# RWKV chunk matrices of one decoder block on TensorE: 64x64 blocks in place of 128x128 block-diagonal ones

## The reference, cut to what matters

```
p = token_shift_lerp(xn @ w_in);  r, k, v, decay, a, kk from p      # 8 heads of 64
def step(S, inp):                                # per head, S is 64x64
    r_t, w_t, k_t, v_t, a_t, b_t = inp           # a_t = -kk, b_t = kk*a
    Sa = einsum('bhvk,bhk->bhv', S, a_t)
    S  = S * w_t + Sa * b_t + v_t * k_t          # outer products
    return S, einsum('bhvk,bhk->bhv', S, r_t)    # y_t
y = scan over 256 tokens
y = (y - mean(y)) * rsqrt(var(y) + LNX_EPS) * lnx_w + lnx_b   # mean and var per head
y = (y + sum(r*k*r_k) * v) * g
merged = sum over 3 branches of sigmoid(xn @ w_gate[b]) * (y_b @ w_branch[b]);  h = x + merged @ w_out
h = h + sparse_moe(rms_norm(h));  out = rms_norm(h)
```

## Time and profile before

| what | value |
|---|---|
| median of 3 runs | 1401.48 us (1398.84 to 1402.33) |
| the profiled execution: span, first to last instruction | 1400.3 us (the page gives no other time for it) |
| TensorE busy | 1345.4 us, 96% of the span |
| VectorE, ScalarE busy | 304.7 us, 199.0 us |
| DMA over the span | 449.68 MB, mean 321 GB/s |
| granted TensorE clock, mean | 0.978 of 2.4 GHz |

### The profile page before, as it was taken

The page is one execution under the profiler, slowest core; times in us unless marked ns, Lnnn a source line. Parts: engine busy times, 40 slices in busy tenths (PEclk is TensorE's granted clock), DMA queues, the critical chain, the costliest instruction groups (busy, mean ns, idle before and its releaser), DMA issues.

```text
span 1400.3 us, 15803 instructions
## 1 busy us (share of the span) xinstructions
PE 1345.4 (96%) x6334; PEld 668.9 (48%) x6334; DVE 304.7 (22%) x477; ACT 199.0 (14%) x382; POOL 0.2 (0%) x4
## 2 busy tenths in 40 slices
PE   7999999999999999999999999999999999999995
PEld 6886799888845333233233333323333333332321
DVE  1256564241111101111011110111201112011112
ACT  1234421110011010011100111001111001110002
POOL 0000000000000000000000000000000000000000
PEclk9999999999997899999999999999999999999998
DMA  9343100159454899999999999999999999999993
GB/s 340 113 169 104 47 1 1 61 185 393 158 203 173 340 417 418 417 416 416 418 418 418 417 418 416 417 418 418 418 418 417 417 418 418 417 419 415 415 416 126
DMA packets 95164, 449.68 MB, mean 321 GB/s; under 512 B 8529, under 2 KB 20945, under 8 KB 62193
## 3 DMA queue, kind: packets, MB, share of 16 engines
q1 hardware_dynamic: 94828, 448.00, 80.0%
q10 hardware_dynamic: 292, 1.07, 0.2%
HBM read 447.99 MB, written 1.05 MB: 321 GB/s over the span
## 4 chain that ended last, share of the span: by engine, by line
PE 87%; DMA 5%; DVE 4%; issue 1%; SPq 1%; ACT 1%; PEldq 0%; DVEq 0%
PE ps L447 84%; DMA ring<-in_w_exp 3%; DMA upper<-in_w_exp 2%; PE ps L906 1%; SPq L412 1%; DVE upper L1414 1%; PE ps L665 1%; SPq L404 1%; DVE ring L1329 0%; PE ps L917 0%; DMA xrows<-in_x 0%; ACT ring L1106 0%; PE ps L463 0%; DVE ring L1419 0%; DVE ring L1420 0%
## 5 line engine op out<-in xcount | busy, mean ns | idle before, releaser
L447 PE MATMUL ps<-ring,upper 128*64 128x512 f32 (+4 forms) x2656 | 604.6, 579 | 10.6 <-PE ps L447 4.3
L447 PEld LDWEIGHTS ps<-ring,upper 128*64 128x64 f32 (+2 forms) x2656 | 207.8, 144 | 379.7 <-issue 362.5
L447 PE MATMUL ps<-upper 128*64 128x512 f32 (+6 forms) x1544 | 287.8, 459 | 7.1 <-PE ps L447 4.3
L447 PEld LDWEIGHTS ps<-upper 128*64 128x64 f32 (+3 forms) x1544 | 145.7, 166 | 144.8 <-issue 136.6
L447 PE MATMUL ps<-xT,ring 128*128 128x256 f32 x672 | 150.7, 382 | 0.0
L447 PEld LDWEIGHTS ps<-xT,ring 128*128 128x128 f32 x672 | 127.2, 191 | 19.3 <-issue 2.3
L1581 DVE TENSOR_TENSOR xrows<-xrows,ps 128x1024 f32<-128x1024 f32 x32 | 39.1, 1221 | 352.2 <-PE ps L447 352.2
L1565 DVE TENSOR_SCALAR upper<-ps 128x512 f32<-128x512 f32 x32 | 22.1, 691 | 420.7 <-PEq L886 420.7
L1204 ACT ACTIVATE upper<-upper 128x512 f32<-128x512 f32 x32 | 20.2, 630 | 536.9 <-DVE upper L1565 536.9
L447 PE MATMUL ps<-merged,cst 1*64 1x512 f32 x256 | 66.2, 633 | 0.0
L1210 ACT ACTIVATE factors<-ps 64x512 f32<-64x512 f32 x64 | 37.9, 591 | 199.5 <-PEq L901 198.8
(11 more groups left out here) (199 smaller groups left out, 521.8 us busy)
## 6 DMA issues: line engine op xcount, KB each, us to landing
ring<-in_w_exp SPq DMA_DIRECT2D x288, 1024.0 KB, 19.3
upper<-in_w_exp SPq DMA_DIRECT2D x96, 1024.0 KB, 19.2
ring<-in_w_gate SPq DMA_DIRECT2D x9, 1024.0 KB, 4.9
ring<-in_w_in SPq DMA_DIRECT2D x8, 896.0 KB, 11.6
ring<-in_w_in SPq DMA_DIRECT2D x8, 640.0 KB, 3.9
ring<-in_w_branch SPq DMA_DIRECT2D x5, 1024.0 KB, 5.1
ring<-in_w_mem_kv SPq DMA_DIRECT2D x4, 1024.0 KB, 4.9
ring<-in_w_out SPq DMA_DIRECT2D x4, 1024.0 KB, 13.2
```

Of the source, the lines that this page charges most:

```text
L447: return pe.matmul(o, l, r, start=start, stop=stop, skip_group_check=True)
```

## The change

The off-diagonal halves are no longer stored or multiplied. Chunk c of a token tile lies on partitions 64c to 64c+63 and every head is a block of 64 columns. Every product of the stage is a 64x64 tile of the array, in an order (`corners`) that goes through the array's four quarters. The inverse's level 0 is transposed by VectorE (32x32 blocks), and so is the last operand before level 5. The state is 64 columns wide. `y` is made in token layout, normed there by VectorE with reductions, then transposed back on TensorE; the norm's weight and bias are applied by ScalarE in the copy from PSUM. `ar` has three parts, so that one matmul gives a x state and r x state together. `WIDE_AT` and the waits of the first DMAs into these slots follow the new layout.

```
-WIDE_AT = (8, 72, 80, 88, 96, 0, 16, 24, 32, 40)
+WIDE_AT = (88, 96, 8, 72, 80, 0, 16, 24, 32, 40)
...
                 elif s == NARROW:
-                    sp.wait_ge(t1_ps, 4 * (LEVELS - 1))
-                elif s == NARROW + 1:
-                    sp.wait_ge(yh_ps, 2)
+                    sp.wait_ge(pv_sb, 4)
+                elif s == NARROW + 2:
+                    sp.wait_ge(xx_ps, 2 * (LEVELS - 1))
+                elif s == NARROW + 3:
+                    sp.wait_ge(y_ps, NCH)
                 elif s == NARROW + 5:
-                    sp.wait_ge(y_rwkv_sb, 1)
+                    sp.wait_ge(y_rwkv_sb, TT)
...                                                    TensorE: gram, own values, inverse
-            for g in range(4):
...
-                    mm(ps[:, n % 6, 0:T], bT[b:b + 64, i, ts], ar[b:b + 64, i, :, ts])
-                    mm(ps[:, n % 6, T:2 * T], kT[b:b + 64, i, ts], ar[b:b + 64, i, :, ts], False).then_inc(gram_ps, 1)
+            corners = ((0, 0), (1, 1), (0, 1), (1, 0))
+            for n in range(4):
+                t, q = n // 2, n % 2
+                for i in range(2):
+                    for x, src in enumerate((bT, kT)):
+                        for a, c in corners:
+                            toks = slice(t * P + c * CH, t * P + (c + 1) * CH)
+                            last = mm(ps[rows64(c), 2 * n + a, (2 * i + x) * P:(2 * i + x + 1) * P],
+                                      src[rows64(a), 2 * q + i, toks], ar[rows64(a), (2 * q + i) * NCH + 2 * t + c, 1:3, :], i == 0 and x == 0)
+                last.then_inc(gram_ps, 1)
+            pe.wait_ge(gram_sb, 2)
+            own_values(0, 0)                 # 16 matmuls 64x64x64
+            pe.wait_ge(gram_sb, 3)
+            pe.wait_ge(inv0_sb, 1)
+            turn_inverse(0)                  # 4 transposes 128x128
+            pe.wait_ge(gram_sb, 4)
+            own_values(1, 6)
+            pe.wait_ge(inv0_sb, 2)
+            turn_inverse(1)
             for j in range(1, LEVELS):
...
+                    for h in range(HP):
+                        for c, a in corners:
+                            last = mm(ps[rows64(a), 2 * t + c, h * 64:(h + 1) * 64], gram[rows64(c), 2 * t + h // 2, a, h % 2, 0, 0, :],
+                                      inv[rows64(c), t, h, a, :], h == 0)
+                    last.then_inc(t1_ps, 1)
                     if j > 1:
+                        turn_inverse(t)
+                for t in range(TT):
+                    pe.wait_ge(t1_sb, 2 * (j - 1) + t + 1)
+                    pe.wait_ge(turned_sb, 2 * (j - 1) + t + 1)
...                                                    16 matmuls again, x = invT_a x t1s
...                                                    TensorE: one chunk of the recurrence
+                if ch:                        # waits: s_sb, and y_sb (invT_sb, twin_sb for ch 1)
+                    for hp in range(HP):
+                        for a in range(2):
+                            last = mm(ps[:, bank + a, hp * 64:(hp + 1) * 64], ar[rows64(a), hp * NCH + ch, 1 - e:3 - e, :],
+                                      state[rows64(a), ch % 2, hp, :], hp == 0)
+                    last.then_inc(r_ps, 1)
+                if ch < NCH - 1:              # 8 matmuls ktok x vtok
                 fill((ch, "a"))
+                for h in range(HR):           # 8 matmuls invT x rs_, 8 gram x vtok
                 fill((ch, "b"))
                 pe.wait_ge(u_sb, ch + 1)
+                if ch < NCH - 1:              # 8 matmuls btok x us, then s_ps
+                for h in range(HR):           # 8 matmuls gram x us, then y_ps
                 fill((ch, "c"))
...
-            fill("mean") ... mm(ps[:, b, :], heads, yT[:, 2 * b:2 * b + 2, :]) ... fill("var") ... mm(ps[:, b, :], heads, sqr[...])
+            fill("norm0")
+            pe.wait_ge(y_sb, 3)
+            pe.wait_ge(ynorm_sb, 1)
+            turn_y(0)                         # 4 transposes
+            fill("norm1")
+            pe.wait_ge(ynorm_sb, 2)
+            turn_y(1)
             fill("rest")
...                                                    VectorE: gram and level 0, last level
+            for n in range(4):
+                dve.wait_ge(gram_ps, n + 1)
+                TTn(gram[:, n]..., ps[:, 2 * n:2 * n + 2, :]..., const("causal")..., ALU.mult).then_inc(gram_sb, 1)
+                link(TTn(base, gram[:, n, :, :, 0, 0, :]..., const("level0t")..., ALU.mult))
+                link(TTn(base..., base..., const("eye")..., ALU.add))
+                if n % 2:
+                    dve.transpose(flat(inv[:, t]), flat(invT[:, t])).then_inc(inv0_sb, 1)
...
+                if j == LEVELS - 2:
+                    for t in range(TT):
+                        step(dve.transpose(flat(invT[:, t]), flat(inv[:, t])))
...                                                    VectorE: norm in token layout
+            def norm(t):
+                dve.wait_ge(y_sb, 2 * t + 2)
+                link(dve.tensor_reduce(stat[:, 3 * t, :], yh, AX.X, ALU.add))
+                link(TS(stat[:, 3 * t, :], stat[:, 3 * t, :], 1.0 / 64, None, ALU.mult))
+                link(TTn(yh, yh, stat[:, 3 * t, :]..., ALU.subtract))
+                link(TTn(sh, yh, yh, ALU.mult))
+                dve.tensor_reduce(stat[:, 3 * t + 1, :], sh, AX.X, ALU.add).then_inc(var_sb, 1)
+                dve.wait_ge(var_root, t + 1)
+                link(dve.reciprocal(stat[:, 3 * t + 2, :], stat[:, 3 * t + 1, :]))
+                TTn(yh, yh, stat[:, 3 * t + 2, :]..., ALU.mult).then_inc(ynorm_sb, 1)
```

More of the change, by code:

```diff
@@ L71 @@
 _at = 0
-for _n, _w in (("ident", P), ("heads", P), ("causal", 2 * P), ("level", LEVELS * P), ("level0t", P), ("before", P),
+for _n, _w in (("ident", P), ("heads", P), ("causal", P), ("level", LEVELS * CH), ("level0t", CH), ("eye", CH), ("before", P),
                ("ones", P), ("dist", 2 * P), ("iota", T), ("resets", T)):
@@ L111, in fill_points @@
 def fill_points():
-    points = [(ch, s) for ch in range(NCH) for s in "abc"] + ["mean", "var", "rest"]
+    points = [(ch, s) for ch in range(NCH) for s in "abc"] + ["norm0", "norm1", "rest"]
     counts = [1] * (3 * NCH) + [2, 3]
@@ L669, in _ @@
[L669 to L681 removed]
+            pe.wait_ge(pv_sb, 4)
@@ L713, in _ @@
[L713 to L720, removed]
+                        if t == 0:
+                            pe.wait_ge(av_sb, 2)
+                    else:
+                        pe.wait_ge(inv_sb, 2 * (j - 2) + t + 1)
@@ L722, in piece @@
+            pe.wait_ge(av_sb, 4)
             def piece(p):
@@ L758, in _ @@
             for ch in range(NCH):
-                t, c = ch // 2, ch % 2
-                rs = slice(64 * c, 64 * c + 64)
+                t, e = ch // 2, ch % 2
+                own, other = rows64(e), rows64(1 - e)
                 toks = slice(ch * CH, (ch + 1) * CH)
+                bank = 2 * (ch % 2)
                 if ch:
                     pe.wait_ge(s_sb, ch)
-                for hp in range(HP):
-                    last = mm(ps[rs, 0, hp * P:(hp + 1) * P], ar[:, hp, 0, toks], state[:, ch % 2, hp, :], hp == 0)
@@ new lines, in _, with turn_y @@
+                for h in range(HR):
+                    last = mm(ps[other, bank + h % 2, (h // 2) * 64:(h // 2 + 1) * 64], gram[own, 2 * t + h // 4, h % 2, h // 2 % 2, 0, 1, :],
+                              us[own, t, h * 64:(h + 1) * 64], False)
+                last.then_inc(y_ps, 1)
+                fill((ch, "c"))
+            def turn_y(t):
+                for f in range(HP):
+                    last = pe.transpose(ps[:, t, f * P:(f + 1) * P], ytok[:, t, f * P:(f + 1) * P], ident)
+                last.then_inc(yT_ps, 1)
@@ L1492, in _ @@
-            merge(after[0])
-            dve.wait_ge(var_root, 1)
-            link(dve.reciprocal(sqr, sqr))
-            link(TTn(yc, yc, sqr, ALU.mult))
-            for f in range(HP):
-                step(TS(yc[:, f, :], yc[:, f, :], col("lnw", f), col("lnb", f), ALU.mult, ALU.add))
-            settle()
-            link(TTn(yc, yc, bonus, ALU.add))
-            TTn(gT, gT, yc, ALU.mult).then_inc(y_rwkv_sb, 1)
-            for m in after[1:] + list(range(N_FILL, len(UNITS))):
+            norm(1)
@@ L1502, in _ @@
+            merges_of("norm0")
+            finish(0)
+            merges_of("norm1")
+            finish(1)
+            after = [p // PIECES for p in points["rest"] if p % PIECES == 5]
+            for m in after + list(range(N_FILL, len(UNITS))):
                 merge(m)
```

336 lines of the change are left out of this document (166 added, 170 removed).

## The result

| | median us | lowest to highest | runs |
|---|---|---|---|
| before | 1401.33 | 1398.84 to 1402.33 | 4 |
| changed | 1353.88 | 1353.18 to 1354.34 | 4 |

The ratio is 0.965 (95% interval 0.961 to 0.969): 47.5 us faster. The prediction had 1378 us and a range from 1363; the gain is twice what was forecast, and outside its range. In a second set of runs the changed kernel had 1351.9 us against 1401.1, ratio 0.964 (0.961 to 0.968). Profiled spans: 1400.3 us before, 1351.4 us after. Over all sets, 6 of the 37 executions of the kernel before took 1410 to 1412 us at a mean granted clock of 0.970 or lower; the medians hardly feel them, but a profile can be of such an execution, as e3's is.

What follows compares the result with a forecast made beforehand. TensorE was taken to bound the kernel until the expert stream restarts. Gram stage and inverse 14.3 plus recurrence 9.1 made 23.4 us, from 1400.3 to 1376.9 us of span, 1378 us median; 8-in-10 range 1363 to 1399.

Steps and rivals of the forecast that it cites:

- What bounds the kernel: TensorE bounds the first half, the expert stream the second; a microsecond saved before the stream's restart is one at the end.
- Gram stage: Gram stage and level 0: VectorE becomes the bound, TensorE needs 6.4 us; level 1 starts at 176.7 us against 180.3.
- The price of a 64x64 tile: Time per record on TensorE: 50 ns for alternating tiles, bounds 30 and 61; 61 for tiles in one row half.
- Inverse: Levels 1 to 5 take 7.4 us each against 9.06; recurrence starts 14.3 us earlier, gram stage's 3.6 included.
- Recurrence: Recurrence and norm: 22.3 us against 31.4 for the changed products, 9.1 us less, bounds 9.7 and 5.6.
- The end of the range: Fast end of the forecast: all tiles at the low ends save 36 us, giving 1365 us; range from 1363.
- Rival 1: Clock falls to 0.50 with small tiles; if held through the inverse, 37 us more, 1415 us; chance 0.08.
- Rivals 2 to 4: No overlap of small tiles, about 1440 us (0.04); half gain, 1393 us (0.12); no change, 1401 us (0.06).
- The floors: Possible floors on TensorE matmul starts: about 25 ns, a level of 4.2 us, or about 62 ns, 8.9 us.

Runs made afterwards that it cites:

- e3: Kernel before, with only the inverse's t1 products as two 64x64 tiles on the diagonal: 1396.1 us against 1401.7, ratio 0.9955; its profiled execution took 1408.0 us.
- e1: Changed kernel with long groups of 64x64 tile matmuls on one, two or four quarters added ahead of the recurrence, results unused: 1397.1 us.
- e5: Changed kernel with six idle products put into TensorE's two waits of the gram stage: 1350.3 us, ratio to before 0.9634.
- e8: Changed kernel with every gram product issued twice in the gram stage: 1352.5 us.
- e9: Changed kernel with half-tile groups and longer quarter groups added ahead of the recurrence: 30 ns a record for the column pair; no total given.
- a0: The changed kernel run once more, unaltered, as base for later runs: 1351.9 us, ratio to before 0.9641.
- e2: Changed kernel with the inverse's loops over quarters and heads swapped, four matmuls in a row on one quarter: 1363.7 us.
- e10: Changed kernel with the quarter order in gram stage and inverse altered so neighbours share a row half: 1355.1 us in one run.
- e4: Changed kernel with the wide slots in the order of before, and the waits that go with it: 1351.4 us, ratio 0.9655.
- e6: Changed kernel with the recurrence's r in four quarters and b'u mixed with the y products: 1350.8 us, ratio to before 0.9639.

## Why the prediction was wrong, step by step

- **What bounds the kernel**: right. Restart and end moved together by 48.0 and 48.9 us; e1 shows the same for 43 us added.
- **Gram stage**: 12.5 us forecast and measured, in part by luck. At full clock the stage lasts 11.8 us (e5); the low clock, which the forecast did not have, added 0.7. That VectorE bounds it was right (e8), TensorE's 6.4 us were too many (3.72 us for its 128 records). VectorE's transposes, which no row had shown, take 0.71 us (I took 0.69, with 3.3 as the far end).
- **The price of a 64x64 tile**: this is the step that failed. It said "Lower end: 118 / 4 = 30 ns. Upper end for alternating tiles: 61, if what I see there is a floor of two instructions a record [...] I take 50". Long runs give 15.9 ns, groups in the kernel 20. Two faults. The 61 ns in the earlier trace rows was the stream of 128 columns over two halves; e9 measures 30 ns on the same halves with 64. And the lower end divided the wrong thing: 118 ns for weights of 64 columns in one half was again the stream of 128 columns. The same form costs 59 with 64 columns, and 59 over four quarters is 15. I had written that load and stream both halve and that neighbours lie in other rows and columns, which is a factor of eight from a full tile's 118, and then divided by four.
- **Inverse**: the mechanism held, the size did not. With 20 ns a level is 2.5 + 1.2 + 0.2 = 3.9 us. The stage is 17.3 us shorter than forecast, of the 25.5 us by which the span beat the forecast gain of 23.4; the pause of 0.9 us (below) is inside.
- **Recurrence**: the same term, 6.3 us of the 25.5. 288 records at 41 ns on the average (11.8 us) in place of 61 (17.6 us); `r` 65 ns against 73. I had put these tiles at 61 because they lie in one half of the rows; but k'v, and `u` with the own y part, go to both column halves, that is to two quarters, where e1 has 30 ns, and they took 39 and 34.
- **The end of the range**: "All tiles at the low ends: 1365 us" took the wrong floor, so the range could not hold 1354.
- **Rival 1, the clock**: the fall exists, but it is short: from 173.4 to 176.6 us in the changed kernel's trace, half a microsecond into level 1, and up to about 178.5 us in a0's. The other levels ran at full clock. It cost about 1 us (e5 against a0).
- **Rivals 2 to 4**: not so. Of TensorE's waits in the inverse the largest is 0.41 us, inside level 5 and behind VectorE's transposes; in the level shown it is 0.15. And the stretch behind the norm is as long as before (144.7 against 145.1 us), so its weights do not come late.
- **The floors**: from "TensorE: Matmul & The Clock Gate" of the Trainium skill (the part on 56 ns against 53.3 ns) I named floors of 25 and 62 ns between starts, with estimates of 4.2 and 8.9 us a level. Neither binds here: 15.9 ns a record, weight load and stream, in four quarters (e1), and 3.93 us a level. Where the page and the measurement differ, the measurement holds. The same page of the Trainium skill has the rule that was missing, in its Part 3: matmuls whose tiles lie in other row and column groups run at the same time, with some 4 ns between starts. e1 agrees in kind (16, 30, 59 ns for four, two, one). In the changed kernel's `u` two records in different quarters start 0.01 us apart (208.89 and 208.90 us), but over a long group no run here has less than 15.4 ns a record.

## What to carry to other kernels

Before taking a price from a row, ask which of load and stream set it, and scale each by its own size: a pace read on 128 moving columns says nothing of 64. On this chip small float32 tiles reached a quarter of one tile's price when four in a row lay in four different quarters; count the matmuls of a group by quarter, since the group cannot be shorter than its fullest quarter (b'u with y), and order them so that neighbours lie in different quarters (e2 shows 46 ns in place of 20 without that). And with a stream that waits for one release, whatever lies ahead of the release counts one to one.

## What the runs showed of the hardware, not expected

**Instruction supply.** At 16 to 20 ns a record TensorE can run out of instructions. In the changed kernel:

```profile
187.20 0.68 PE L451 MATMUL ps<-ring,upper 64*64 64x64 f32 x27
188.77 0.34 PE L451 MATMUL ps<-ring,upper 64*64 64x64 f32 x5 [0.89 <-issue]
```

A group of 32 is cut in two with 0.89 us between, and nothing that the profile shows released it; in e9 the same comes after 257 records of the long group, for 1.14 us. In e10 the same group of the program is cut at the same place, 27 and 5, for 0.45 us; in a0, e4, e6 and e8 it is not cut. The only DMAs from 186 to 190 us in the changed kernel are two of the instruction queue, 0.03 MB together. That it is the fetch of instructions was not tried; it is my reading.

**The clock in busy stretches.** In e9, with TensorE never waiting but for that 1.14 us, the granted clock went from full (2.4 GHz) to 0.50 (1.2 GHz) in the group of four quarters with 16 columns. It was full up to 223.0 us and 0.50 from there, so it fell inside the pause, which lies from 222.42 to 223.56 us:

```profile
218.46 3.96 PE L451 MATMUL ps<-upper 64*64 64x16 f32 x257
223.56 7.07 PE L451 MATMUL ps<-upper 64*64 64x16 f32 x255 [1.14 <-issue]
```

```profile
220.00:224.00 4.00, 2.86 (x182) 2.82 (x180) 0.00 (x0) 0.00 (x0) 0.00 (x0) 0.88 0.01 4
224.00:228.00 4.00, 4.00 (x156) 4.00 (x156) 0.00 (x0) 0.00 (x0) 0.00 (x0) 0.50 0.01 4
```

It stayed there through 20.7 us of records on one quarter with 64 columns, 108 ns each, though in e1 the same kind of group, entered at full clock, kept it for 7.6 us. In e1 it fell 3.5 us into the last group (one quarter, 16 columns), with no wait at all. Nor does it take small tiles. In e3's profiled execution it fell 2.6 us into the gram stage, which is that of the kernel before (64x128 weights, 256 moving columns), and stayed low with TensorE busy all the time (columns as in the earlier trace rows):

```profile
166.00:190.00 24.00, 24.00 (x63) 17.58 (x62) 13.32 (x21) 1.19 (x2) 0.00 (x0) 0.50 0.00 0
```

From gram start to level 1 it took 27.3 us in place of 16.1; these 11.2 us are nearly all of the 11.9 by which the execution is above e3's median. The kernel before, profiled at full clock, does the same work there, so what starts the fall stays open. So rival 1 is a real danger, and it was one before the change too; in the changed kernel's gram stage the fall cost about 1 us.
